# Projecting the v_s columns with the first chunk of w_in instead of with the last

## The chip, the core and the metric

The kernel runs on one core of a Trainium2 chip. The metric is the device time of one execution, in microseconds (us), as the median of several runs. TensorE is called PE here (PEld for its weight loads), VectorE DVE, ScalarE ACT, GpSimd POOL and SyncE SP.

## The reference, cut to what matters

Two transformer blocks over 512 tokens of width 1024: a block with sparse attention (NSA) and a gated MLP mixer plus a dense feed-forward part, then a block with differential attention and a mixture of 32 experts. The change concerns only the input projection of the first block:

```python
h = rms_norm(x, norm_mix_pre)                    # 512 x 1024
proj = jnp.einsum("bsd,de->bse", h, w_in)        # w_in is 1024 x 2328
q, k_c, v_c, k_s, v_s, k_w, v_w, gate_logits, u, v = jnp.split(proj, points, axis=-1)
# columns: q 0-511, k_c 512-639, v_c 640-767, k_s 768-895, v_s 896-1023,
#          k_w 1024-1151, v_w 1152-1279, gates 1280-1303, u 1304-1815, v 1816-2327
```

k_c and v_c are then compressed by small MLPs, and k_s, v_s, k_w, v_w and the gates go into the attention, with bias tables built from rel_bias.

## The kernel before

**Precision and splits.** Each fp32 operand is split into a high and a low fp32r part. ScalarE rounds a weight chunk from the ring buffer RING into WH (`act_split`), VectorE subtracts to get WL (`dve_split`), and PE sums three matmuls into a bank of PSUM (`pe_mm3`, L255 to L257: high x high, high x low, low x high).

**Chunks.** The weights of everything ahead of the experts come as a list of chunks (`front_chunks`). A chunk holds 4 k-tiles (512 of the 1024 rows) of some columns, so each set of columns is two chunks, which sum into the same banks. SyncE loads them in order into three slots of RING (`sp_load`, L218); a slot is reused when the chunk three before has been split (semaphore `w_lo`), or, for the raw chunks of the compression weights, when PE has consumed it (`p_blk`). Three pairs of WH and WL buffers hold the split chunks; a split waits for PE to have finished with the chunk that had the buffer (`p_pr`).

**The stage around the change** (`pe_win`, `act_win`, `dve_win`). The order on each engine is written out by hand. PE takes chunk 0 and 1 (k_c, v_c, k_s), 2 and 3 (q), 4 and 5 (k_w, then v_s, v_w and the gates), then the raw chunks 6 to 9 (L749: the compression's first layer), then 10 and on (u and v).

`pe_project` has two kinds of outputs. For kind "w" the weights are the stationary operand and the 512 tokens stream past: an output is 128 columns of w_in, transposed, and takes 4 k-tiles x 3 matmuls of 512 columns per chunk. For the other kind a block of 128 tokens is stationary and the weights stream: an output is 128 tokens x the columns, and takes 4 x 3 matmuls of as many columns as the set has. In chunks 4 and 5 the four outputs of the second kind have 280 columns: v_s, v_w and the gates (24).

**Biases.** The bias tables are made by tiny matmuls of 8 columns in bank 7: one far, four near groups of 64 (L627), four compressed groups of 31 (L634). `pe_project` takes a function `behind` that PE calls after each output; the bias groups stand there. A group waits until VectorE has copied the one before out of bank 7 (`v_bf`, L643; `v_bc`, L650).

**Leaving the banks.** ScalarE copies k_c and v_c out (L780) and starts DMAs that lay them out, copies k_s (L786, into KT4), starts more DMAs, splits chunks 4 and 5, and copies q (L799, bank 3 last) and k_w. VectorE copies v_s, v_w and gates together (L876, VSG). The first output of chunk 4 is k_w in bank 3, and waits for the last copy of q.

Of the kernel before, what the change touches and what calls it, by code (L numbers as in the profile page):

```python
# [59 lines left out]
def front_chunks():  # L60

    out = []

    def columns(src, cols, nout, nk=8, gain=None):
        for k0 in range(0, nk, 4):
            out.append(Chunk(src, k0, 4, cols, nout, gain=gain))

    def both(src, rows):
        for k0, nk in rows:
            for half in range(2):  # L70
                out.append(Chunk(src, k0, nk, [(512 * half, 512)], 4))

    columns("w_in", [(512, 384)], 3)
    columns("w_in", [(0, 512)], 4)
    columns("w_in", [(1024, 128), (896, 128), (1152, 152)], 5)
    for nm in ("cmp_w1_k", "cmp_w1_v"):
        for c in range(2):
            out.append(Chunk(nm, 8 * c, 8, [(0, 256)], 0, raw=True))
    columns("w_in", [(1304, 512)], 4)
    columns("w_in", [(1816, 512)], 4)  # L80
    both("w_out", ((4, 4), (0, 4)))
    for f in range(11):
        columns("w_gate_up", [(256 * f, 256), (FF + 256 * f, 256)], 4, gain=8)
    both("w_down", DOWN_ROWS)
    for grp in (0, 1, 3, 2):
        columns("w_in_2", [(grp * 512, 512)], 4, gain=16)
    both("w_out_2", ((4, 4), (0, 4)))

    loaded, outs, split, at, users = [0] * 3, 0, 0, 0, []
    for c, ch in enumerate(out):
        loaded[c % 3] += 16
        ch.slot, ch.loaded = c % 3, loaded[c % 3]
        ch.first_out = outs
        outs += ch.nout
        ch.done = outs
        ch.at, at = at, at + 128 * ch.nk * ch.w
        ch.split = None  # L100
        if not ch.raw:
            ch.split = split
            split += 1
            back = 3
            if ch.src == "w_out_2":
                if c == len(out) - 4:
                    users.append((users[-3][0], outs + 4))
                back = 2 if c == len(out) - 2 else 3
            ch.buf, ch.after = users[-back] if len(users) >= 3 else (split - 1, None)
            if c == len(out) - 1:  # L110
                ch.buf, ch.after = None, None

            users.append((ch.buf, outs + 2 if c == 16 else outs))
    return out
# [11 lines left out]
def program(nc, A):  # L126
    ctx = ExitStack()
    with ctx:
# [39 lines left out]
        def cols(off, a, n):  # L168
            return ar(off, a * n).rearrange("p (a n) -> p a n", a=a)
# [14 lines left out]
        for parts in (  # L184

                (("p_gt", 1), ("p_bf", 5), ("p_bc", 4)),

                (("p_kc", 1), ("p_vc", 1), ("p_gm", 8)),

                (("a_kct", 2), ("a_kts", 1), ("a_q", 4), ("a_kw", 1), ("a_hid", 2), ("a_sg", 1), ("a_u", 4), ("a_v", 4), ("a_lnv", 4)),  # L190

                (("a_lam", 1), ("a_rope", 2), ("a_sr", 1), ("a_gk", 1)),

                (("v_li", 1), ("v_gk", 1), ("v_ct", 1), ("v_cmpb", 1), ("v_eov", 1), ("v_sel", 1), ("v_blm", 1), ("v_dst", 1)),

                (("v_lam", 2), ("v_ang", 1), ("v_sr", 1)),

                (("v_gt", 1), ("v_t3", 1), ("v_bf", 5), ("v_bc", 4), ("v_blk", 8), ("v_vw", 4), ("v_hidr", 1), ("v_kc", 1), ("v_vc", 1), ("v_lnm", 1), ("v_wst", 2), ("v_zv", 1), ("v_gm", 8)),
        ):
            before = 0  # L200
            for name, count in parts:
                AT[name] = before
                before += count
# [316 lines left out]
        KT4 = cols(o, 4, 512); o_kt = o; o += 2048  # L520
        U = cols(o, 4, 512); o_u = o; o += 2048
        V = cols(o, 4, 512); o_v = o; o += 2048
        VSG = cols(o, 4, 280); o += 1120
        VS, VWG = VSG[:, :, 0:128], VSG[:, :, 128:280]
        BC = ar(o, 1024).rearrange("p (i h c) -> p i h c", i=4, h=8); o += 1024
        WK = ar(o, 3072); o_wk = o; o += 3072
        KC = ar(o, 64); o += 64
# [88 lines left out]
        def pe_bias_far(e):  # L616
            e.wait_ge(s("v_win"), AT["v_t3"] + 1)
            e.wait_ge(s("d_tb"), 64)
            e.wait_ge(s("v_xt"), XT["mix"] + 8)
            e.matmul(PS[7][:, 496:504], OH2[0:97, 711:712].broadcast_to([97, 128]), T3[0:97, 24:32], start=True, stop=True  # L620
                     ).then_inc(s("p_tab"), 1)
# [85 lines left out]

        def pe_win(e):
            xt = xt_of("mix")
            outs = [(n, PS[n][:, :], "w", n * 128, 128) for n in range(3)]  # L710
            pe_project(e, 0, outs, XP, 0, 8, {n: [("v_xt", XT["mix"] + n + 1)] for n in range(3)}, xt)

            def biases(e, o):
                if o == 0:
                    pe_bias_far(e)
                else:
                    pe_bias_near(e, o - 1)

            def more_biases(e, o):
                if o < 2:  # L720
                    pe_bias_near(e, o + 2)
                else:
                    pe_bias_cmp(e, o - 2)

            pe_project(e, 1, outs, XP, 4, 8, {}, xt, behind=biases)
            outs = [(m, PS[m][:, :], "w", m * 128, 128) for m in range(4)]
            free = {0: [("a_win", AT["a_kct"] + 1)], 1: [("a_win", AT["a_kct"] + 2)], 2: [("a_win", AT["a_kts"] + 1)]}

            def last_biases(e, o):
                if o < 2:  # L730
                    pe_bias_cmp(e, 2 + o)

            pe_project(e, 2, outs, XP, 0, 8, free, {}, behind=more_biases)
            pe_project(e, 3, outs, XP, 4, 8, {}, {}, behind=last_biases)
            outs = [(3, PS[3][:, :], "w", 0, 128)] + [(4 + i, PS[4 + i][:, 0:280], i, 128, 280) for i in range(4)]
            free = {3: [("a_win", AT["a_q"] + 4)], 7: [("v_win", AT["v_bc"] + 4)]}
            pe_project(e, 4, outs, XP, 0, 8, free, {})
            pe_project(e, 5, outs, XP, 4, 8, {}, {})

            for n in range(2):  # L740
                e.wait_ge(s("v_win"), AT["v_blk"] + 4 * n + 4)
                for c in (6 + 2 * n, 7 + 2 * n):
                    e.wait_ge(s(f"w_ld{CH[c].slot}"), CH[c].loaded)
                    for m in range(2):
                        if c % 2 == 0:
                            e.wait_ge(*((s("a_win"), AT["a_q"] + 1 + 2 * n + m), (s("a_win"), AT["a_kw"] + 1))[n * m])
                        for k in range(8):
                            k0 = 8 * (c % 2) + k
                            x = e.matmul(PS[2 * n + m][:, 0:62].rearrange("p (g c) -> p g c", g=2),  # L749
                                         RING[:, CH[c].slot, k * 256 + m * 128:k * 256 + (m + 1) * 128],  # L750
                                         BLK[n][:, k0, :, 0:31], start=(k0 == 0), stop=(k0 == 15))
                    x.then_inc(s("p_blk"), 1)

            def compressed_u(e, o):
                if o == 0:
                    pe_cmp_keys(e)
                elif o >= 2:
                    pe_cmp_logits(e, o - 2)

            def compressed_u2(e, o):  # L760
                if 1 <= o:
                    pe_cmp_values(e, o - 1)
                pe_cmp_T(e, o)
                if o < 2:
                    pe_cmp_logits(e, o + 2)

            def compressed_v(e, o):
                if o == 0:
                    pe_cmp_values(e, 3)

            pe_project(e, 10, full(H1), XP, 0, 8, {4 + i: [("v_win", AT["v_vw"] + 1 + i)] for i in range(4)}, {}, behind=compressed_u)
            pe_project(e, 11, full(H1), XP, 4, 8, {}, {}, behind=compressed_u2)
            pe_project(e, 12, full(H1), XP, 0, 8, {4 + i: [("a_win", AT["a_u"] + 1 + i)] for i in range(4)}, {}, behind=compressed_v)
            pe_project(e, 13, full(H1), XP, 4, 8, {}, {})

        def act_win(e):
# [7 lines left out]
                        e.dma_start(KK[n][64 * par:64 * par + 64, g, :], KCT[n][64 * g:64 * g + 64, :]).then_inc(s(f"d_kk{n}"), 16)  # L784
            e.wait_ge(s("p_pr"), CH[1].first_out + 3)
            e.activation(KT4[:, 0, :], PS[2][:, :], ACT.Copy).then_inc(s("a_win"), 1)  # L786
            e.wait_ge(s("a_win"), AT["a_kts"] + 1)
            for half in range(2):
                e.dma_start(KT4[64 * (1 - half):64 * (1 - half) + 64, 1, :], KT4[64 * half:64 * half + 64, 0, :]
                            ).then_inc(s("d_kts"), 16)  # L790
# [62 lines left out]
        def dve_win(e):  # L853
# [8 lines left out]
                                        ).then_inc(s("v_win"), 1)  # L862

            dve_bias_far(e)
            dve_split(e, 3)
            for kb in range(4):
                dve_bias_near(e, kb)
            for i in range(4):
                dve_bias_cmp(e, i)
# [3 lines left out]
            dve_split(e, 5)  # L873
            for i in range(4):
                e.wait_ge(s("p_pr"), CH[5].first_out + 2 + i)
                e.tensor_copy(VSG[:, i, :], PS[4 + i][:, 0:280]).then_inc(s("v_win"), 1)  # L876
            for n in range(2):
                e.memset(HID[n][:, :, :, 31:32], 0.0).then_inc(v_c.sem, v_c.up())
            e.memset(VC, 0.0).then_inc(v_c.sem, v_c.up())
# [2235 lines left out]
```

## Time and profile before

| | |
|---|---|
| median of 3 runs | 2118.25 us (2116.45 to 2121.68) |
| the profiled execution: its time | 2118.25 us |
| its span | 2116.4 us |
| PE busy | 2060.8 us (97%) |
| DVE busy | 1537.0 us (73%) |
| ACT busy | 1383.2 us (65%) |
| mean granted PE clock | 0.994 of full |
| all DMA | 511.27 MB, mean 242 GB/s |

Read it so: the span is from the first to the last instruction in the profile; the time has some 1.85 us around it. Busy is time with at least one instruction under way. Matmuls overlap, so a busy PE is not a PE at its peak, and the distance from one matmul's start to the next says more than a matmul's own duration. The stage of the change lies in the first 100 us.

### The profile page before, as it was taken

The page shows a single profiled execution, that of the slowest core. Times are in us where ns is not written, and L with a number is a line of the kernel's source. Part 1 is how long each engine was busy: PE and PEld are TensorE (multiplying, and loading weights), DVE is VectorE, ACT ScalarE, POOL GpSimd, SP SyncE. Part 2 cuts the span into 40 slices and gives each one's busy share as a digit, 9 for nine tenths or more (in the row PEclk, how much of TensorE's full clock was granted, in tenths as well). Part 3 has the DMA queues.
Part 4 walks back from the last instruction along what each step waited for, and adds up shares of the span by engine and source line. Part 5 has one row for each costly group of instructions (what it writes and reads, how often), then busy time and mean ns, then how long its engine had stood idle before and what let it go on. Part 6 is the DMA issues. An engine that isn't in the chain of part 4 may idle for free.

```text
span 2116.4 us, 31589 instructions
## 1 busy us (share of the span) xinstructions
PE 2060.8 (97%) x10497; PEld 1707.9 (81%) x10497; DVE 1537.0 (73%) x1825; ACT 1383.2 (65%) x1870; POOL 194.8 (9%) x232
## 2 busy tenths in 40 slices
PE   7998899999999999899999999999999999999998
PEld 6887788888887887778888888888888888888877
DVE  4357743332325677789899999989898989898984
ACT  3247643222323447478888888888888888888863
POOL 0000000000000000111111111111111111111110
PEclk9999999999999999999999999999999999999999
DMA  6321013222323311489999999999999999999971
GB/s 199 135 71 61 21 55 124 87 94 80 120 100 103 117 72 41 171 307 373 369 372 367 370 369 371 369 366 375 366 379 363 370 372 372 361 371 371 376 264 40
DMA packets 86560, 511.27 MB, mean 242 GB/s; under 512 B 17285, under 2 KB 18905, under 8 KB 29146
## 3 DMA queue, kind: packets, MB, share of 16 engines
q1 hardware_dynamic: 71312, 487.61, 61.2%
q0 software_dynamic: 9680, 17.33, 3.2%
q10 hardware_dynamic: 5498, 5.39, 0.9%
q8 instruction: 45, 0.74, 0.1%
q14 instruction: 25, 0.20, 0.0%
HBM read 503.44 MB, written 23.07 MB: 249 GB/s over the span
## 4 chain that ended last, share of the span: by engine, by line
PE 91%; DVE 5%; issue 1%; ACT 1%; DMA 1%; ACTq 0%; POOL 0%; DVEq 0%; SPq 0%; POOLq 0%
PE PS L2595 17%; PE PS L2597 17%; PE PS L2596 17%; PE PS L255 10%; PE PS L257 10%; PE PS L256 10%; PE PS L2478 1%; PE PS L2592 1%; PE PS L2605 1%; PE PS L1153 1%; PE PS L1865 1%; DVE AR L1124 1%; PE PS L1082 0%; PE PS L1800 0%; PE PS L1793 0%
## 5 line engine op out<-in xcount | busy, mean ns | idle before, releaser
L2472 DVE TENSOR_TENSOR WL<-RING,WH 128x2048 fp32r<-128x2048 f32 x385 | 873.5, 2288 | 95.6 <-ACT WH L2452 92.5
L2452 ACT ACTIVATE WH<-RING 128x1024 fp32r<-128x1024 f32 x770 | 806.4, 1059 | 163.1 <-PE PS L2597 157.5
L2595 PE MATMUL PS<-WH,RA 128*128 128x512 f32 x1540 | 628.5, 408 | 0.0
L2597 PE MATMUL PS<-WH,RA 128*128 128x512 f32 x1540 | 600.7, 390 | 0.0
L2596 PE MATMUL PS<-WL,RA 128*128 128x512 f32 x1540 | 600.4, 390 | 0.0
L2597 PEld LDWEIGHTS PS<-WH,RA 128*128 128x128 f32 x1540 | 289.5, 188 | 61.7
L2596 PEld LDWEIGHTS PS<-WL,RA 128*128 128x128 f32 x1540 | 289.9, 188 | 58.1
L2595 PEld LDWEIGHTS PS<-WH,RA 128*128 128x128 f32 x1540 | 290.8, 189 | 55.3
L255 PE MATMUL PS<-WH,RA 128*128 128x512 f32 (+1 forms) x560 | 219.4, 392 | 3.4 <-DVE WL L245 2.2
L257 PE MATMUL PS<-WH,RA 128*128 128x512 f32 (+1 forms) x560 | 216.1, 386 | 0.0
L256 PE MATMUL PS<-WL,RA 128*128 128x512 f32 (+1 forms) x560 | 215.8, 385 | 0.0
L250 DVE SCALAR_TENSOR_TENSOR WL<-RING,GT,WH 128x512 fp32r<-128x512 f32 x120 | 82.2, 747 | 167.7 <-ACT WH L235 167.6
L235 ACT ACTIVATE WH<-RING,GT 128x512 fp32r<-128x512 f32 x120 | 76.8, 713 | 175.2 <-PE PS L257 175.2
L255 PE MATMUL PS<-RA,WH 128*128 128x512 f32 (+1 forms) x448 | 168.7, 377 | 3.3 <-DVE RA L458 1.6
L256 PE MATMUL PS<-RA,WH 128*128 128x512 f32 (+1 forms) x448 | 167.6, 374 | 0.0
L257 PE MATMUL PS<-RA,WL 128*128 128x512 f32 (+1 forms) x448 | 167.6, 374 | 0.0
L245 DVE TENSOR_TENSOR WL<-RING,WH 128x2048 fp32r<-128x2048 f32 (+3 forms) x29 | 62.3, 2150 | 92.0 <-ACT WH L230 91.8
L255 PEld LDWEIGHTS PS<-WH,RA 128*128 128x128 f32 x560 | 105.7, 189 | 24.1 <-DVE WL L245 2.3
L257 PEld LDWEIGHTS PS<-WH,RA 128*128 128x128 f32 x560 | 105.7, 189 | 21.2
L256 PEld LDWEIGHTS PS<-WL,RA 128*128 128x128 f32 x560 | 105.8, 189 | 20.2 <-issue 0.2
L230 ACT ACTIVATE WH<-RING 128x2048 fp32r<-128x2048 f32 (+3 forms) x29 | 52.1, 1801 | 105.5 <-PE PS L257 95.9
L2757 POOL DMA_INDIRECT acc_scr<-AR,SMALL x32 | 69.9, 2185 | 464.8 <-issue 464.8
(395 smaller groups left out, 2265.9 us busy)
## 6 DMA issues: line engine op xcount, KB each, us to landing
RING<-w_experts SPq DMA_DIRECT2D x390, 1024.0 KB, 7.3
RING<-w_front SPq DMA_DIRECT2D x58, 1024.0 KB, 4.9
X<-x SPq DMA_DIRECT2D x4, 512.0 KB, 5.6
acc_scr<-X SPq DMA_DIRECT2D x4, 512.0 KB, 5.0
xs_scr<-AR SPq DMA_DIRECT2D x4, 512.0 KB, 3.1
X<-acc_scr SPq DMA_DIRECT2D x4, 512.0 KB, 5.5
out<-X SPq DMA_DIRECT2D x8, 256.0 KB, 2.0
RING<-w_front SPq DMA_DIRECT2D x2, 816.0 KB, 4.4
```

The costliest lines, as they stand in the source:

```text
L235: x = e.activation(WH[:, ch.buf, v], RING[:, ch.slot, v], ACT.Copy, scale=GT[:, g:g + 1])
L245: x = e.tensor_tensor(WL[:, ch.buf, 0:n], RING[:, ch.slot, 0:n], WH[:, ch.buf, 0:n].bitcast(F32), ALU.subtract)
L250: x = e.scalar_tensor_tensor(WL[:, ch.buf, v], RING[:, ch.slot, v], GT[:, g:g + 1], WH[:, ch.buf, v].bitcast(F32), ALU.mult, ALU.subtract)
L255: e.matmul(out, a[0], b[0], start=start, stop=False)
L256: e.matmul(out, a[0], b[1], start=False, stop=False)
L257: return e.matmul(out, a[1], b[0], start=False, stop=stop)
L2452: e.activation(WH[:, m % 3, v], RING[:, m % 6, v], ACT.Copy).then_inc(s("m_hi"), 1)
L2472: e.tensor_tensor(WL[:, m % 3, :], RING[:, m % 6, :], WH[:, m % 3, :].bitcast(F32), ALU.subtract).then_inc(s("m_lo"), 1)
L2595: e.matmul(PS[bank][:, :], lhs[0][:, kr + k, :], WH[:, m % 3, c], start=(sel is None and kr == 0 and k == 0), stop=False)
L2596: e.matmul(PS[bank][:, :], lhs[0][:, kr + k, :], WL[:, m % 3, c], start=False, stop=False)
L2597: x = e.matmul(PS[bank][:, :], lhs[1][:, kr + k, :], WH[:, m % 3, c], start=False, stop=(stop and k == 3))
L2757: e.indirect_dma_start(acc_d, bass.IndirectOffsetOnAxis(TCOL, 0), YY, None, bounds_check=511, oob_is_err=False, compute_op=ALU.add).then_i ...
```

## The change

The v_s columns (896 to 1023) move into chunks 0 and 1, which grow from 384 to 512 columns; chunks 4 and 5 shrink from 408 to 280. Chunks 0 and 1 get four more outputs each, of the second kind, 128 columns wide, in banks 3 to 6. The outputs of that kind in chunks 4 and 5 shrink from 280 to 152 columns (v_w and the gates). Chunk 1 now has seven outputs, and seven of the bias groups stand behind them (far, four near, two compressed); the last two compressed ones stand behind chunk 2. ScalarE copies v_s out in four copies after that of k_s; VectorE's copies in chunk 5 are 152 wide. VectorE copies the first near group before it splits chunk 3. VS and VWG are now tiles of their own.

```diff
-    columns("w_in", [(512, 384)], 3)
+    columns("w_in", [(512, 512)], 7)
     columns("w_in", [(0, 512)], 4)
-    columns("w_in", [(1024, 128), (896, 128), (1152, 152)], 5)
+    columns("w_in", [(1024, 280)], 5)
...
-(("a_kct", 2), ("a_kts", 1), ("a_q", 4), ...
+(("a_kct", 2), ("a_kvs", 5), ("a_q", 4), ...
...
-        VSG = cols(o, 4, 280); o += 1120
-        VS, VWG = VSG[:, :, 0:128], VSG[:, :, 128:280]
+        VS = cols(o, 4, 128); o += 512
+        VWG = cols(o, 4, 152); o += 608
...
-            outs = [(n, PS[n][:, :], "w", n * 128, 128) for n in range(3)]
-            pe_project(e, 0, outs, XP, 0, 8, {n: [("v_xt", XT["mix"] + n + 1)] for n in range(3)}, xt)
+            outs = ([(n, PS[n][:, :], "w", n * 128, 128) for n in range(3)]
+                    + [(3 + i, PS[3 + i][:, 0:128], i, 384, 128) for i in range(4)])
+            pe_project(e, 0, outs, XP, 0, 8, {n: [("v_xt", XT["mix"] + n + 1)] for n in range(7)}, xt)

             def biases(e, o):
                 if o == 0:
                     pe_bias_far(e)
+                elif o < 5:
+                    pe_bias_near(e, o - 1)
                 else:
-                    pe_bias_near(e, o - 1)
-
-            def more_biases(e, o):
-                if o < 2:
-                    pe_bias_near(e, o + 2)
-                else:
-                    pe_bias_cmp(e, o - 2)
+                    pe_bias_cmp(e, o - 5)
...
-            free = {0: [("a_win", AT["a_kct"] + 1)], 1: [("a_win", AT["a_kct"] + 2)], 2: [("a_win", AT["a_kts"] + 1)]}
+            free = {0: [("a_win", AT["a_kct"] + 1)], 1: [("a_win", AT["a_kct"] + 2)], 2: [("a_win", AT["a_kvs"] + 1)], 3: [("a_win", AT["a_kvs"] + 2)]}
...
-            pe_project(e, 2, outs, XP, 0, 8, free, {}, behind=more_biases)
-            pe_project(e, 3, outs, XP, 4, 8, {}, {}, behind=last_biases)
-            outs = [(3, PS[3][:, :], "w", 0, 128)] + [(4 + i, PS[4 + i][:, 0:280], i, 128, 280) for i in range(4)]
-            free = {3: [("a_win", AT["a_q"] + 4)], 7: [("v_win", AT["v_bc"] + 4)]}
+            pe_project(e, 2, outs, XP, 0, 8, free, {}, behind=last_biases)
+            pe_project(e, 3, outs, XP, 4, 8, {}, {})
+            outs = [(3, PS[3][:, :], "w", 0, 128)] + [(4 + i, PS[4 + i][:, 0:152], i, 128, 152) for i in range(4)]
+            free = {4 + i: [("a_win", AT["a_kvs"] + 3 + i)] for i in range(3)}
+            free.update({3: [("a_win", AT["a_q"] + 4)], 7: [("v_win", AT["v_bc"] + 4)]})
...
             e.activation(KT4[:, 0, :], PS[2][:, :], ACT.Copy).then_inc(s("a_win"), 1)
-            e.wait_ge(s("a_win"), AT["a_kts"] + 1)
+            for i in range(4):
+                e.wait_ge(s("p_pr"), CH[1].first_out + 4 + i)
+                e.activation(VS[:, i, :], PS[3 + i][:, 0:128], ACT.Copy).then_inc(s("a_win"), 1)
+            e.wait_ge(s("a_win"), AT["a_kvs"] + 1)
...
             dve_bias_far(e)
+            dve_bias_near(e, 0)
             dve_split(e, 3)
-            for kb in range(4):
+            for kb in range(1, 4):
                 dve_bias_near(e, kb)
...
-                e.tensor_copy(VSG[:, i, :], PS[4 + i][:, 0:280]).then_inc(s("v_win"), 1)
+                e.tensor_copy(VWG[:, i, :], PS[4 + i][:, 0:152]).then_inc(s("v_win"), 1)
```

## Rows read from the trace of the kernel before

**Rows 1.** The page's chain that ended last: share of the span by engine.

```profile
PE 91%; DVE 5%; issue 1%; ACT 1%; DMA 1%; ACTq 0%; POOL 0%; DVEq 0%; SPq 0%; POOLq 0%
```

**Rows 2.** Chain that ended last, 0 to 120 us: start, us, engine, tile, line.

```profile
18.31 0.47 PE PS L255
...
67.33 0.61 ACT AR L799
68.08 0.47 PE PS L255
...
86.22 7.10 PE PS L749 x64
93.34 4.98 DMA RING<-w_front
98.35 1.92 ACT WH L230
100.29 2.30 DVE WL L245
102.64 0.80 PE PS L255
103.43 0.43 PE PS L256
...
108.71 0.89 PE PS L931 x8
```

**Rows 3.** Timeline of PE, chunks 4 and 5: start, us, line, tile, shapes.

```profile
70.92 0.28 PE L255 MATMUL PS<-WH,RA 128*128 128x280 f32 x1
...
77.09 0.40 PE L255 MATMUL PS<-RA,WH 128*128 128x512 f32 x1
77.32 0.39 PE L256 MATMUL PS<-RA,WH 128*128 128x512 f32 x1
```

**Rows 4.** Timeline of PE, transposes of an expert.

```profile
926.11 0.60 PE L2605 MATMUL PS<-CST,AR 128*128 128x128 f32 x4
```

**Rows 5.** Timeline of PE, two fp32r matmuls of 128 columns in the attention.

```profile
162.14 0.22 PE L1147 MATMUL PS<-RA 128*128 128x128 f32 x1
162.20 0.28 PE L1148 MATMUL PS<-RA 128*128 128x128 f32 x1
```

**Rows 6.** Weight loads by line and form: count | busy us, mean ns.

```profile
L256 PEld LDWEIGHTS PS<-WL,RA 128*128 128x128 f32 x560 | 105.8, 189 | 20.2 <-issue 0.2
...
L749 PEld LDWEIGHTS PS<-AR,RING 128*128 128x128 f32 x128 | 14.4, 192 | 0.0
...
L627 PEld LDWEIGHTS PS<-AR 97*128 97x128 bf16 x256 | 6.7, 96 | 1.0 <-issue 1.0
```

**Rows 7.** Timeline around the first near-bias group.

```profile
32.20 1.76 PE L627 MATMUL PS<-AR 97*128 97x8 bf16 x64
...
33.82 0.48 PE L255 MATMUL PS<-RA,WH 128*128 128x512 f32 x1
...
34.09 0.68 DVE L643 COPY RING<-PS 128x512 f32<-128x512 f32 x1
```

**Rows 8.** Timeline of VectorE, its split of chunk 4.

```profile
66.04 1.86 DVE L245 TENSOR_TENSOR WL<-RING,WH 128x1632 fp32r<-128x1632 f32 x1
```

**Rows 9.** DMA issues between 2.9 and 3.3 us: count, KB, us to landing.

```profile
RING<-w_front SPq DMA_DIRECT2D x1, 768.0 KB, 8.1
```

**Rows 10.** Timeline of VectorE, first activation tiles.

```profile
17.42 5.36 DVE L334 SCALAR_TENSOR_TENSOR RA<-PS,GT,RA 128x512 fp32r<-128x512 f32 x8 [1.60 <-ACT RA L327]
```

**Rows 11.** Stretches: engines busy (x instructions), PEclk, DMA share, GB/s.

```profile
86.00:93.30 7.30, 7.30 (x68) 7.30 (x66) 0.96 (x4) 0.00 (x0) 0.00 (x0) 1.00 0.37 120
...
98.20:101.60 3.40, 2.26 (x21) 2.12 (x20) 1.31 (x1) 3.00 (x4) 0.00 (x0) 1.00 0.86 299
101.60:108.40 6.80, 5.76 (x15) 4.65 (x16) 3.61 (x3) 5.32 (x5) 0.00 (x0) 0.50 0.86 318
```

More of the change, by code:

```diff
@@ L188, in program @@
                 (("p_kc", 1), ("p_vc", 1), ("p_gm", 8)),
-                (("a_kct", 2), ("a_kts", 1), ("a_q", 4), ("a_kw", 1), ("a_hid", 2), ("a_sg", 1), ("a_u", 4), ("a_v", 4), ("a_lnv", 4)),
+                (("a_kct", 2), ("a_kvs", 5), ("a_q", 4), ("a_kw", 1), ("a_hid", 2), ("a_sg", 1), ("a_u", 4), ("a_v", 4), ("a_lnv", 4)),
                 (("a_lam", 1), ("a_rope", 2), ("a_sr", 1), ("a_gk", 1)),
```

## The prediction

> **What bounds the kernel now.** I read the page first: the chain that ended last is 91% PE [rows 1]. So what matters is whether the edited stretch lies on that chain, and there the chain in order of time is the view to read [rows 2]. From 18.31, the first matmul of chunk 0, it runs through PE alone to 93.34, with one step aside: at 67.33 ScalarE reads bank 3 (0.61 us) before chunk 4 may write it. At 86.22 begin the compression matmuls of L749. When they have consumed the ring's chunk 7, SyncE issues the load of chunk 10 (4.98 us), ScalarE and VectorE split it (1.92 and 2.30 us), and PE goes on at 102.64. The reader should see two things. The load that holds PE up at 93 to 103 us is itself started by PE, so PE work added before 86.22 moves everything behind it one for one. And no other engine has to be made faster here: up to 93.34 the chain never passes through VectorE.
>
> Then I read single matmuls, start to start, because their busy times overlap. 512 columns go at 0.23 us. The 48 matmuls of 280 columns go from 70.92 to 77.09, which is 6.17 / 48 = 0.1285 us each [rows 3]. The 280-column ones are in the "x" outputs of chunks 4 and 5, where activations are the stationary operand: a new 128x128 weight load for each.
>
> **The change part by part.** (a) v_s (128 columns of w_in) moves from chunks 4 and 5 to chunks 0 and 1. The bytes over the six chunks, and the columns computed, are the same. But the matmuls are not: before, v_s shared its matmuls with v_w and the gates (280 columns). After, chunks 0 and 1 get 4 outputs x 4 k-tiles x 3 terms x 2 chunks = 96 more matmuls of 128 columns, and the 96 of 280 columns become 96 of 152. PE issues 96 more weight loads and as many matmuls, for no more columns.
>
> What a narrow fp32r matmul with a new weight tile costs is the disputed price; the trace has no long row of them. Plain fp32 instructions with new 128x128 weights go at 7.10 / 64 = 0.111 us with 62 columns, 0.89 / 8 = 0.111 us with 64 columns [rows 2], and 4 transposes of 128 columns take 0.60 us [rows 4], of which 0.28 is the time of the last by itself (a lone 128-column matmul's in [rows 5]): (0.60 - 0.28) / 3 = 0.11 us. Width makes no difference there, so something other than the streamed columns sets 0.111. The weight load is the candidate: its record is 192 ns for fp32 and 189 ns for the fp32r loads of the projection, but 96 ns for bf16 [rows 6], and bf16 pairs go at 1.60 / 64 = 0.025 us, as the near-bias group of L627 shows [rows 2]. fp32r weights load like fp32 weights, so I take 0.111 us for 128 and for 152 columns. The ends: from above 0.1285, since fewer columns with the same load should not take longer than 280 do. From below 0.06: in the attention one fp32r matmul of 128 columns is followed by another with other weights after 162.20 - 162.14 = 0.06 us [rows 5]. That is a single pair after a 512-column matmul, whose length hid the first load, so it does not show a stream; the long rows are nearer to the case.
>
> Added: 96 x 0.111 = +10.7 us. Saved: 96 x (0.1285 - 0.111) = -1.7 us. Net +9.0 us on PE. With 0.1285 for both it is +12.3.
>
> A rule of the Trainium skill would price this lower: TensorE: Matmul & The Clock Gate, section Back-to-back issue gap, gives about 81 ns for each pair of weight load and matmul at 128 columns in a sustained stream. By it the sum would be 96 x 0.081 - 96 x (0.1285 - 0.081) = +3.2 us. The fp32 rows at 0.111 us speak against it; no row here shows it for fp32r.
>
> (b) The bias matmuls are re-hung. The far one, four near and four compressed groups still run, each as long as before: behind chunks 1 and 2 rather than 1, 2 and 3. Their PE time is unchanged (a near group is 33.82 - 32.20 = 1.62 us [rows 7]). What could be new is a wait for bank 7: VectorE must copy a group away before the next. The copy begins at 34.09 and ends at 34.77, 0.95 us after the group made way for L255 at 33.82 [rows 7]. Before, an output of 12 x 0.23 = 2.7 us stood between groups; now, from the fourth output on, an output of 12 narrow matmuls does, 12 x 0.111 = 1.33 us. That still covers 0.95, so I cost it at 0. If the narrow ones ran at 0.06 the cover would be 0.72 us, and some 0.25 us would be lost at each of three hand-offs. VectorE's first near copy is moved ahead of its split of chunk 3 for this; that split is wanted only when chunk 3 begins, with all of chunk 2, 48 x 0.23 = 11 us, still between.
>
> (c) ScalarE copies v_s out of banks 3 to 6, four copies of 128 columns (0.61 us is what it takes for 512 [rows 2]), between chunk 1's outputs. Queued behind them on its queue are two key-copy DMAs, three loads of the compression's second weights, and the split of chunk 4. The split's WL half is wanted by PE when chunk 4 starts, with chunks 2 and 3 between, 96 x 0.23 = 22 us; the DMAs' data later. Cost 0. Chunk 2 writes bank 3 as its fourth output, long after that bank's copy.
>
> (d) The wait before chunk 4. Chunk 4 starts at 68.08, because of the bank 3 copy (67.33 + 0.61). VectorE's split of chunk 4 ended at 66.04 + 1.86 = 67.90 [rows 8], as late as the copy. After the change this split is earlier (the last bias copy before it is two outputs further ahead of chunk 3, and the chunk is smaller), but the bank stays: chunk 4 still writes bank 3 first. Gain 0; at most 0.9 us if both went.
>
> (e) The start. Chunks 0 and 1 grow from 768 KB to 1 MB each. Chunk 0 is issued at about 3.0 and lands 8.1 us later, at 11.1 [rows 9]. Behind x (2 MB) it came at no less than (2 + 0.75) MB in 11.1 us, so 256 KB more are at most 1.0 us. Its split is the first step that could feel it. VectorE's split of 512 columns more (2048 take 2.30 us [rows 2]) adds 0.6 us, and VectorE idled 1.60 us between this split and its first activation tile at 17.42 [rows 10]. I take it as hidden; if the load and both splits (0.5 us on ScalarE too) all came on top, 2.1 - 1.6 = 0.5 us would show.
>
> **Sum.** +10.7 - 1.7 + 0 = +9.0 us. The profiled execution took 2118.25 us (span 2116.4 and 1.85 around it), which is also the median of the three runs, so 2127.3 us, 0.43% more. About 0.3% (6.4 us) is what a measurement of this kernel can tell from no change.
>
> **The rivals.** Partly covered loads: the spacing is between the two ends, say (0.06 + 0.111) / 2 = 0.085 us, because part of a load runs under the matmul ahead. Then 96 x 0.085 = 8.2, less 96 x (0.1285 - 0.085) = 4.2: +4.0 us, 2122.3. The one pair at 0.06 is for it; the groups at 0.111 are against. The 81 ns of the Trainium skill's page TensorE: Matmul & The Clock Gate would make this the case.
>
> Narrow matmuls at stream rate, which is the case on the other side (not slower): 0.06 us for 128 columns and 0.06 x 152 / 128 = 0.071 for 152. Added 5.8, saved 96 x 0.0575 = 5.5, hand-offs 0.75: +1.1 us, 2119.3. It decides from a spacing of 0.098 us down, where 96 x (2 x spacing - 0.1285) falls under the 6.4 us named above. For it speaks the same pair, against it the equal 0.111 at 62, 64 and 128 columns.
>
> The clock falls in the new stretch. Around chunk 1's last outputs PE would now do nothing but bias groups of 8 columns and narrow matmuls for some 9 us. The granted clock was 1.00 at 86 to 93.3, nearly all 62-column instructions, but 0.50 (1.2 of 2.4 GHz) at 101.6 to 108.4, behind 98.2 to 101.6 in which PE was busy 2.26 of 3.40 us with such instructions [rows 11]. At 0.50 the 512-column matmuls go at 0.43 us rather than 0.23 [rows 2], and about 13 of them passed before the clock came back: 13 x 0.20 = 2.6 us. So +11.6 us, 2129.9. Against: the clock stayed at 1.00 under seven us of 62-column work [rows 11]. The spell at 101.6 itself could also shift or vanish, 2.6 us less: 2124.7; this belongs to the spread of the forecast.
>
> The added work is hidden: the sum would be 0 if something else ended last in this stretch. The chain passes through nothing but PE from 18.31 to 67.33 and again from 68.08 to 93.34 [rows 2], so I give it almost nothing.
>
> **Numbers.** Forecast (0.111 us, spread 2124.7 to 2130): 0.65. Clock falls: 0.12. Partly covered: 0.10. Stream rate: 0.10. Anything else, a gain in a later stage included: 0.03. The range 2120.5 to 2131 takes in all but the stream-rate case and the outliers. Slower by over 0.3%: nearly all of the first, all of the second, a little of the third, 0.76. Within: 0.20. Faster: 0.04.
>
> **What would show it.** In the trace after: 96 matmuls of 128 columns in chunks 0 and 1 spaced 0.11 us, so chunk 1 begins about 48 x 0.111 = 5.3 us later; L749's 64-group begins at about 95.3 rather than 86.22, chunk 10's first matmul at about 111.7. The 152-column ones are spaced 0.11 too. No PE wait over 0.1 us on VectorE's bias copies; granted clock 1.00 between 16 and 95 us. The prediction is wrong if the spacing of the 128-column matmuls is under 0.09 us, if PE waits at bank 7 or for a split, or if the distance of 9 us between the two traces at L749 is gone by the end.

## The result, and the profile after

The changed kernel takes 2136.1 us (median of 4 runs, 2132.85 to 2138.85) against 2119.47 (2116.45 to 2121.68): ratio 1.0081, 95% interval 1.0065 to 1.0096, so 14 to 20 us slower. A second comparison gave 1.0075 (1.006 to 1.009). I had forecast 9.0 us, with 2131 as the upper end of the range.

The page of the kernel after: the chain that ended last is PE's as before [rows 1].

```profile
PE 91%; DVE 4%; issue 2%; DMA 1%; ACT 1%; ACTq 0%; POOL 0%; SPq 0%; DVEq 0%; POOLq 0%
```

The chain in order of time, to be held against [rows 2]:

```profile
18.11 0.47 PE PS L255
...
42.02 1.60 PE PS L627 x64
45.01 1.60 PE PS L627 x64
...
49.27 1.73 PE PS L627 x64
...
57.99 0.63 PE PS L255
58.62 0.43 PE PS L256
...
64.45 0.23 PE PS L256
...
84.21 0.61 ACT AR L800
...
101.42 7.15 PE PS L747 x64
108.58 5.23 DMA RING<-w_front
...
118.13 0.79 PE PS L255
```

L747 (L749 before) begins at 101.42 instead of 86.22: 15.2 us late, where I expected 9. The distance is made by then, ahead of the load of chunk 10 and everything behind it; chunk 10's first matmul, at 118.13, is 15.5 us late. The row to stop at is 58.62: a 512-column matmul of chunk 2 that takes 0.43 us, and it is back to 0.23 at 64.45.

The stretches of the kernel after (columns as in [rows 11]) say why:

```profile
16.20:46.60 30.40, 29.45 (x335) 25.72 (x333) 17.50 (x24) 12.34 (x15) 0.00 (x0) 1.00 0.51 150
46.60:63.80 17.20, 17.20 (x199) 15.71 (x199) 2.28 (x5) 1.97 (x4) 0.00 (x0) 0.51 0.13 28
63.80:101.40 37.60, 36.82 (x250) 31.96 (x246) 12.05 (x15) 5.42 (x7) 0.00 (x0) 1.00 0.20 64
```

The granted clock is 1.00 to 46.6, about 0.5 for 17.2 us (the 1.2 GHz level), and 1.00 again up to L747. PE is busy all through the middle stretch. In the kernel before, the clock is 1.00 throughout this part:

```profile
26.50:48.00 21.50, 21.50 (x323) 18.00 (x322) 9.06 (x17) 5.27 (x5) 0.00 (x0) 1.00 0.67 193
48.00:67.20 19.20, 19.20 (x194) 15.46 (x192) 6.69 (x11) 3.36 (x4) 0.00 (x0) 1.00 0.00 1
```

The narrow matmuls, on PE's timeline in chunk 0 of the kernel after. They answer to [rows 3] and [rows 5]:

```profile
26.40 0.22 PE L255 MATMUL PS<-WH,RA 128*128 128x128 f32 x1
26.46 0.28 PE L256 MATMUL PS<-WL,RA 128*128 128x128 f32 x1
26.57 0.27 PE L257 MATMUL PS<-WH,RA 128*128 128x128 f32 x1
26.68 0.27 PE L255 MATMUL PS<-WH,RA 128*128 128x128 f32 x1
...
31.71 0.45 PE L255 MATMUL PS<-RA,WH 128*128 128x512 f32 x1
```

48 matmuls of 128 columns take 31.71 - 26.40 = 5.31 us, 0.111 us each. The first pair stands 0.06 us apart, just as the pair of [rows 5] did, and from the second on it is 0.11: such a pair behind a wide matmul did not show what a run of them costs.

The hand-off of bank 7, on the timeline of the kernel after, the counterpart of [rows 7]:

```profile
41.86 1.76 PE L627 MATMUL PS<-AR 97*128 97x8 bf16 x64
...
43.48 0.31 PE L255 MATMUL PS<-WH,RA 128*128 128x128 f32 x1
...
43.65 0.69 DVE L643 COPY RING<-PS 128x512 f32<-128x512 f32 x1 [1.43 <-PE PS L627]
...
44.85 1.76 PE L627 MATMUL PS<-AR 97*128 97x8 bf16 x64
```

The near group at 41.86 gives way to a narrow output at 43.48, VectorE's copy runs from 43.65 to 44.34, and the next group starts at 44.85, when that output is through. PE never waits for the bank.

### The profile page after: what moved, and what is told of

It is laid out like the page before. It is cut to its first block, busy times and chain, and to the rows that moved or that the text cites. A ratio compares the mean times of both kernels' runs of the same rounds, so it can differ in the third digit from the quotient of the medians.

```text
span 2138.6 us, 31785 instructions
## 1 busy us (share of the span) xinstructions
PE 2081.3 (97%) x10593; PEld 1727.7 (81%) x10593; DVE 1537.0 (72%) x1825; ACT 1384.6 (65%) x1874; POOL 194.7 (9%) x232
## 4 chain that ended last, share of the span: by engine, by line
PE 91%; DVE 4%; issue 2%; DMA 1%; ACT 1%; ACTq 0%; POOL 0%; SPq 0%; DVEq 0%; POOLq 0%
PE PS L2597 16%; PE PS L2599 16%; PE PS L2598 16%; PE PS L255 10%; PE PS L257 10%; PE PS L256 10%; PE PS L2480 1%; PE PS L2594 1%; PE PS L2607 1%; PE PS L1155 1%; PE PS L1867 1%; DVE AR L1126 1%; PE PS L1084 1%; DMA AR<-ffn_norm 0%; PE PS L1795 0%
## 5 line engine op out<-in xcount | busy, mean ns | idle before, releaser
L2599 PEld LDWEIGHTS PS<-WH,RA 128*128 128x128 f32 x1540 | 289.6, 188 | 61.8
L2597 PEld LDWEIGHTS PS<-WH,RA 128*128 128x128 f32 x1540 | 290.9, 189 | 57.6 <-issue 2.2
L2598 PEld LDWEIGHTS PS<-WL,RA 128*128 128x128 f32 x1540 | 290.2, 188 | 58.2
L255 PE MATMUL PS<-WH,RA 128*128 128x512 f32 (+2 forms) x592 | 229.4, 387 | 3.6 <-DVE WL L245 2.4
L257 PE MATMUL PS<-WH,RA 128*128 128x512 f32 (+2 forms) x592 | 226.0, 382 | 0.0
L256 PE MATMUL PS<-WL,RA 128*128 128x512 f32 (+2 forms) x592 | 225.8, 382 | 0.0
L255 PEld LDWEIGHTS PS<-WH,RA 128*128 128x128 f32 x592 | 113.6, 192 | 24.5 <-DVE WL L245 2.6
L257 PEld LDWEIGHTS PS<-WH,RA 128*128 128x128 f32 x592 | 113.7, 192 | 21.1
L256 PEld LDWEIGHTS PS<-WL,RA 128*128 128x128 f32 x592 | 113.8, 192 | 20.2 <-issue 0.2
L245 DVE TENSOR_TENSOR WL<-RING,WH 128x2048 fp32r<-128x2048 f32 (+2 forms) x29 | 62.3, 2150 | 92.8 <-ACT WH L230 92.7
L230 ACT ACTIVATE WH<-RING 128x2048 fp32r<-128x2048 f32 (+2 forms) x29 | 52.1, 1802 | 110.7 <-PE PS L257 101.6
```

The costliest lines, as they stand in the source:

```text
L245: x = e.tensor_tensor(WL[:, ch.buf, 0:n], RING[:, ch.slot, 0:n], WH[:, ch.buf, 0:n].bitcast(F32), ALU.subtract)
L255: e.matmul(out, a[0], b[0], start=start, stop=False)
L256: e.matmul(out, a[0], b[1], start=False, stop=False)
L257: return e.matmul(out, a[1], b[0], start=False, stop=stop)
L2597: e.matmul(PS[bank][:, :], lhs[0][:, kr + k, :], WH[:, m % 3, c], start=(sel is None and kr == 0 and k == 0), stop=False)
L2598: e.matmul(PS[bank][:, :], lhs[0][:, kr + k, :], WL[:, m % 3, c], start=False, stop=False)
```

## The experiments

Each is told by where its run of L747's 64 instructions begins (86.22 before, 101.42 after), by the granted clock up to there, and by its ratio to the kernel before. The first four share one set of runs of the kernel before, the other four another. The first matmul of chunk 0 does not start at the same time in every trace (18.31 before); where that matters, it is said.

**The biases where they were, the narrow matmuls kept.** On the changed kernel, with `more_biases` as it was before the change:

```diff
-                elif o < 5:
-                    pe_bias_near(e, o - 1)
-                else:
-                    pe_bias_cmp(e, o - 5)
+                elif o < 3:
+                    pe_bias_near(e, o - 1)
...
-            pe_project(e, 2, outs, XP, 0, 8, free, {}, behind=last_biases)
-            pe_project(e, 3, outs, XP, 4, 8, {}, {})
+            pe_project(e, 2, outs, XP, 0, 8, free, {}, behind=more_biases)
+            pe_project(e, 3, outs, XP, 4, 8, {}, {}, behind=last_biases)
```

> The changed kernel with its bias groups back where they were before the change: far and two near groups behind the wide outputs of chunk 1, the others behind chunks 2 and 3; the 96 added matmuls of 128 columns stay. Theory A (two costs: the added weight loads, 9.0 us, and a clock spell of about 6 us that comes from narrow matmuls and bias groups standing side by side): the granted clock stays at 1.00 up to L747, whose 64-group begins near 95.3 us (before 86.2, after 101.4), and the time is 9 to 10 us over the kernel before, near 2128. Rival B (the clock falls from the narrow matmuls alone, wherever the biases are): a stretch at 0.50 in chunk 0 or 1 again, L747 near 99 to 101, time near 2134. Rival C (the loss of 15 us has nothing to do with the order of the biases): L747 at 101, time as the changed kernel's 2136.

Measured: 2129.96 us, median of 6 runs (one of them took 2141.94), ratio 1.0058 (1.0038 to 1.0079). Its chain and its stretches:

```profile
78.81 0.47 PE PS L255
...
102.45 5.61 DMA RING<-w_front
```

```profile
26.50:48.00 21.50, 21.50 (x253) 19.41 (x253) 8.58 (x14) 4.38 (x7) 0.00 (x0) 1.00 0.53 154
48.00:79.00 31.00, 30.22 (x360) 24.96 (x360) 9.12 (x14) 5.11 (x8) 0.00 (x0) 1.00 0.08 17
79.00:95.30 16.30, 16.30 (x122) 15.25 (x122) 5.14 (x8) 1.88 (x2) 0.00 (x0) 1.00 0.46 146
95.30:102.50 7.20, 7.20 (x67) 7.20 (x66) 0.83 (x4) 0.05 (x1) 0.00 (x0) 1.00 0.37 117
```

The clock is 1.00 in all four stretches, and the load of chunk 10 starts at 102.45 instead of 93.34: 9.1 us later. Chunk 4 starts at 78.81 instead of 68.08, 10.7 us later, which is the forecast's term for the added matmuls; the narrower chunks 4 and 5 give 1.6 back. The order of the biases alone is worth 6 us of the 15; with it undone, what is left is the 9.0 us of the forecast.

**The weight loads alone.** The kernel before, with every 280-column matmul issued as one of 128 and one of 152 columns:

```diff
+                if cw == 280:
+                    for k in range(ch.nk):
+                        n = n0 + k
+                        for q0, qw in ((0, 128), (128, 152)):
+                            i = pe_mm3(e, out[:, q0:q0 + qw], ..., n == 0 and q0 == 0, n == nk - 1 and q0 > 0)
```

> The kernel before with each of its 96 matmuls of 280 columns issued as one of 128 and one of 152 with the same weights loaded twice, in chunks 4 and 5, with no bias group near: the added weight loads alone. Theory A (each narrow fp32r matmul with its weight load takes 0.111 us): 96 x (2 x 0.111 - 0.1285) = 9.0 us more, L749 at 95.2 instead of 86.2, clock 1.00 up to there, time near 2128. Rival B (narrow matmuls in a long run bring the clock down by themselves; here 192 of them, 21 us, run on end into the 62-column ones): L749 at 95 but a stretch at 0.50 in it, 100 us or later, time 2131 to 2140. Rival C (a second matmul on the same weights is cheaper): under 5 us.

Measured: 2129.51 us, ratio 1.005 (1.0036 to 1.0064). Its chain, where L759 is the old L749:

```profile
95.25 7.14 PE PS L759 x64
102.41 5.17 DMA RING<-w_front
```

L759 begins at 95.25, 9.03 us later than before; 96 x (2 x 0.111 - 0.1285) is 8.98. This is the cost of chunks 4 and 5 alone, for chunk 4 starts at 68.06 here and at 68.08 before. The clock was 1.00 from 68 to 102 us. In that time 96 narrow matmuls ran on end for 10.7 us, then the 12 of 512 columns with which chunk 5 begins (81.58 to 84.4), then 96 narrow ones again and the 62-column ones; the expectation overlooked the wide ones between. So 96 more weight loads cost 9 us in either place, and a run of 96 narrow matmuls by itself did not bring the clock down. A single run of all 192, as rival B has it, was not tried.

**More columns for nothing.** The changed kernel with its 128-column matmuls widened to 256, of which half is used:

```diff
-                    + [(3 + i, PS[3 + i][:, 0:128], i, 384, 128) for i in range(4)])
+                    + [(3 + i, PS[3 + i][:, 0:256], i, 256, 256) for i in range(4)])
...
-                e.activation(VS[:, i, :], PS[3 + i][:, 0:128], ACT.Copy).then_inc(s("a_win"), 1)
+                e.activation(VS[:, i, :], PS[3 + i][:, 128:256], ACT.Copy).then_inc(s("a_win"), 1)
```

> The changed kernel with its 96 matmuls of 128 columns widened to 256 (k_s and v_s together; the v_s half is used), bias groups as in the changed kernel. More columns stream for nothing. Theory A (the clock falls because the array streams little in that stretch): each matmul takes 0.120 us instead of 0.111, 0.9 us more, but the granted clock stays at 1.00 or falls for less, L747 between 96 and 100 instead of 101.4, time 2129 to 2134, less than the changed kernel's 2136. Rival B (the number of weight loads or of instructions brings the clock down, not the columns): a stretch of 17 us at 0.50 as before, L747 at 102.5 to 104, time 2137 or more.

Measured: 2131.09 us, ratio 1.005 (1.0038 to 1.0063), where the changed kernel has 1.0081 and 1.0075. Its chain, its stretches, and two matmuls on its timeline:

```profile
95.96 7.15 PE PS L747 x64
```

```profile
32.00:60.00 28.00, 28.00 (x458) 24.90 (x457) 8.66 (x10) 5.95 (x9) 0.00 (x0) 1.00 0.35 93
60.00:96.00 36.00, 35.22 (x232) 30.61 (x231) 11.62 (x15) 5.41 (x7) 0.00 (x0) 1.00 0.21 66
```

```profile
45.06 0.28 PE L257 MATMUL PS<-WH,RA 128*128 128x256 f32 x1
45.18 0.28 PE L255 MATMUL PS<-WH,RA 128*128 128x256 f32 x1
```

The matmuls take 0.12 us instead of 0.111, the bias groups stand exactly where the change puts them, and the clock stays at 1.00. L747 begins at 95.96: 0.7 us behind the run with the split 280s, and 5.5 us ahead of the changed kernel. Work that is thrown away made the stage faster. The medians lie 5 to 6 us apart too; the interval lies below the changed kernel's first one and just touches the second. The number of instructions and of weight loads is that of the changed kernel (rival B of this run is out); what differs is that the 96 matmuls stream twice the columns and stand 0.12 us apart. There is one trace of this kernel, but its six runs have mean clocks of 0.991 to 0.994 against 0.985 to 0.991 of the changed kernel. The width of single instructions is not the whole account: the 62-column ones keep 1.00 in every trace here.

**Biases in a run, no narrow fp32r matmuls.** The kernel before, with three near and two compressed groups behind chunk 1's last output (the last two compressed ones behind chunk 2, and VectorE's first near copy ahead of its split of chunk 3, both as in the change):

```diff
-                else:
-                    pe_bias_near(e, o - 1)
+                elif o == 1:
+                    pe_bias_near(e, 0)
+                else:
+                    for kb in range(1, 4):
+                        pe_bias_near(e, kb)
+                    for i in range(2):
+                        pe_bias_cmp(e, i)
```

> The kernel before (no v_s move, no added matmuls) with near groups 1 to 3 and compressed groups 0 and 1 in one run behind chunk 1's last output. PE waits for VectorE's copy of bank 7 between them, about 1 us four times, 4 us. Theory A (bias groups in a run bring the clock down even without narrow fp32r matmuls): a stretch at 0.50 from about 42 us on, chunk 2's first matmuls of 512 columns at 0.43 us, L749 at 90 plus 2 to 5 us. Rival B (it takes the narrow fp32r matmuls): clock 1.00, L749 at 90, time near 2122.

Measured: 2125.64 us, ratio 1.0029 (1.0019 to 1.0039). Its chain and its stretches:

```profile
48.27 0.43 PE PS L256
...
92.77 7.10 PE PS L748 x64
```

```profile
36.00:40.00 4.00, 3.21 (x105) 2.82 (x105) 1.56 (x2) 0.60 (x1) 0.00 (x0) 0.99 0.80 199
40.00:53.70 13.70, 10.92 (x203) 9.12 (x199) 2.28 (x5) 1.56 (x1) 0.00 (x0) 0.51 0.28 75
53.70:73.00 19.30, 19.30 (x116) 15.93 (x113) 12.13 (x12) 3.37 (x4) 0.00 (x0) 1.00 0.30 103
```

The clock falls here too, at 40.0 for 13.7 us, without one narrow fp32r matmul. PE stands idle 0.8 + 2.8 = 3.6 us in the first two stretches (the hand-offs of bank 7), and the 12 matmuls of chunk 2's first output go at 0.43 us, 2.4 us more; L748 is 92.77 - 86.22 = 6.5 us late. So the narrow fp32r matmuls are not needed for a fall (rival B of this run is out). But PE was idle for part of the time here, which it was not in the changed kernel, and no run shows the bias groups without these waits.

**VectorE's order.** The changed kernel with chunk 3's split ahead of the first near copy again:

```diff
-            dve_bias_near(e, 0)
             dve_split(e, 3)
-            for kb in range(1, 4):
+            for kb in range(4):
```

> The changed kernel with VectorE's order of before: chunk 3's split ahead of the first near copy. Theory (this edit is a hand-off detail): PE waits up to about 2 us more for bank 7 at the second near group (split of 2.3 us ahead of the copy, less the 2.7 us output between), nothing else; the spell at 0.50 stays, L747 between 101 and 104. Rival (the edit is part of the loss): L747 earlier than 101.

One run, 2141.07 us. Its chain:

```profile
101.31 7.15 PE PS L747 x64
```

101.31 against 101.42, with the spell (the stretch at the lower clock) in place: in this one trace the edit is worth nothing, not even the wait that I had allowed for. The second near group starts at 41.74, right behind its output (41.86 in the changed kernel).

**The changed kernel once more.** No edit.

> The changed kernel itself once more, as the control of this call and for a second trace. Theory (the spell belongs to the kernel's order of work and comes in every run, as the clock means of 0.986 to 0.991 in its seven runs suggest): again a stretch at 0.50 that begins between 43 and 48 us and ends by 65, L747 near 101; ratio to the kernel before 1.0065 to 1.0096. What differs after 850 us between the first two traces (5 us in the router stage) is a spell that varies from run to run, so the distance to before at the end should not be 22 us again. Rival (the spell was an accident of one execution): clock 1.00 to L747, L747 at 95, time near 2128.

Measured: 2137.17 us, ratio 1.0075 (1.006 to 1.009). Its stretches:

```profile
32.00:45.00 13.00, 13.00 (x214) 11.14 (x214) 5.97 (x4) 3.06 (x5) 0.00 (x0) 0.99 0.56 151
45.00:62.00 17.00, 17.00 (x203) 15.79 (x200) 2.28 (x5) 1.97 (x4) 0.00 (x0) 0.50 0.16 38
62.00:100.00 38.00, 37.22 (x267) 32.25 (x265) 12.04 (x15) 5.41 (x7) 0.00 (x0) 1.00 0.20 63
```

```profile
100.36 7.15 PE PS L747 x64
```

The spell comes again, from 45 to 62, and before it PE was busy 13.00 of 13.00 us. L747 is 14.1 us late; the first matmul stands at 17.21 here, 1.1 us ahead of before, so from there to L747 it is 15.2. The seven runs of the changed kernel in the first comparison have mean clocks of 0.986 to 0.991, and the six here 0.985 to 0.991; the kernel before has 0.990 to 0.995 in its 32 runs of the two calls. The spell belongs to the kernel, not to one execution. At its end this trace lies 20.6 us behind the one of before; I had expected it not to be 22 us again.

**The same work, thinned.** The changed kernel with near groups 2 and 3 behind the second and fourth narrow output, none behind the first and third, and all compressed groups behind chunk 2:

```diff
-                elif o < 5:
+                elif o < 3:
                     pe_bias_near(e, o - 1)
-                else:
-                    pe_bias_cmp(e, o - 5)
+                elif o % 2 == 0:
+                    pe_bias_near(e, o // 2)
...
-                if o < 2:
-                    pe_bias_cmp(e, 2 + o)
+                pe_bias_cmp(e, o)
```

> The changed kernel with its last four narrow outputs of chunk 1 less crowded: near groups 2 and 3 behind the second and the fourth of them, none behind the first and the third, and all four compressed groups behind chunk 2's outputs. Between the second and the last wide output of the stage PE still does only narrow work, 5.3 us of matmuls and 3.2 us of bias groups instead of 5.3 and 4.8. Theory (too little streamed in a stretch brings the clock down; less bias work between narrow matmuls means less of it): no spell or one of 3 to 7 us, L747 at 95.3 to 98. Rival (any mixture of narrow matmuls with bias groups does it): a spell as long as before, L747 at 100 or later.

Measured: 2133.29 us, ratio 1.0066 (1.0051 to 1.0082). Its chain and stretches:

```profile
97.31 7.15 PE PS L746 x64
```

```profile
42.00:49.60 7.60, 7.60 (x161) 7.60 (x158) 1.38 (x2) 1.38 (x4) 0.00 (x0) 0.99 0.48 159
49.60:56.40 6.80, 6.80 (x81) 6.05 (x81) 0.76 (x2) 1.41 (x2) 0.00 (x0) 0.51 0.33 71
56.40:97.00 40.60, 39.82 (x332) 34.18 (x331) 12.84 (x17) 5.41 (x7) 0.00 (x0) 1.00 0.18 59
```

A spell of 6.8 us instead of 17, and L746 at 97.31, 11.1 us late: 9 for the loads, 2 for the clock. With less bias work between the narrow outputs there is less of the spell, as the trace shows; the time's interval overlaps that of the changed kernel. The edit also brings chunk 2's wide matmuls forward, to 52.8 from 57.9, so this run does not tell a less crowded stretch from a shorter one.

**A version that uses the gap.** Built on the kernel before, v_s left where it was: the compressed bias groups run behind L749's last group, where PE waits for chunk 10, in banks 0 and 1; k_w goes to bank 7 and the last 280-column output to bank 3. VectorE copies the compressed groups out after its split of chunk 6.

```diff
+        VB = (4, 5, 6, 3)
...
-            outs = [(3, PS[3][:, :], "w", 0, 128)] + [(4 + i, PS[4 + i][:, 0:280], i, 128, 280) for i in range(4)]
+            outs = [(7, PS[7][:, :], "w", 0, 128)] + [(VB[i], PS[VB[i]][:, 0:280], i, 128, 280) for i in range(4)]
...
                     x.then_inc(s("p_blk"), 1)
+            for i in range(4):
+                pe_bias_cmp(e, i)
```

> Built on the kernel before, with v_s left where it was. The four compressed bias groups run where PE waits for chunk 10 anyway (behind L749's last group, in banks 0 and 1), and k_w goes to bank 7 instead of bank 3, so that chunk 4 need not wait for the copy of q. Theory: 3.1 us of bias groups and 0.4 us of restarts leave the path ahead of L749, the wait of 0.9 us before chunk 4 goes, and about 0.9 us comes back at chunk 10, since the groups take 3.1 us and the gap has 2.2. Sum: L749 begins at 86.2 - 4.4 = 81.8 us, chunk 10 at 102.6 - 3.5 = 99.1, and the time is about 3.5 us under the kernel before, 2115.7, which is within what a measurement can tell. Rival (the spell at 0.50 around chunk 10 gets longer, as PE now does 8-column work just before it): chunk 10's distance is eaten up again, time as before.

Measured: 2115.65 us, median of 11 runs, against 2119.54: ratio 0.9982, 95% interval 0.9973 to 0.9991. Its chain and PE's timeline:

```profile
81.46 14.24 PE PS L744 x128
...
98.86 0.63 PE PS L255
```

```profile
95.53 3.32 PE L635 MATMUL PS<-AR 97*128 97x8 bf16 x124
98.72 0.77 PE L255 MATMUL PS<-WH,RA 128*128 128x512 f32 x1
```

L744 begins at 81.46 (4.8 us earlier than before), the four compressed groups take 3.3 us from 95.53, and chunk 10 starts at 98.86 instead of 102.64, 3.8 us earlier. Of both, 0.3 us is an earlier first matmul (17.99), which leaves 4.4 and 3.5 as expected. The spell around chunk 10 is as long as before, 6.8 us at 0.50 from 97.6, so the rival of this run is out. The gain of 0.18% is small but its interval does not reach 1, and it is the only kernel of these that beats the one before. The two edits were not run apart.

## Why the prediction was wrong

- **The chain lies in PE alone, so work added ahead of L749 moves everything:** right. The 15.2 us at L747 are 15.5 at chunk 10, and still 15.2 at the last matmul of L1802 (866.2 us; 851.0 before, as L1800); in the run with the biases back, 9.1 us at the load behind L751.
- **(a) 0.111 us for a narrow fp32r matmul with new weights, +9.0 us:** right. Chunk 0's 48 took 0.111 us each; the split of the 280s alone cost 9.03 us, and the changed kernel without the spell 9.1. The rivals of partly covered loads and of the stream rate are out. For the rule of the Trainium skill weighed there (TensorE: Matmul & The Clock Gate, Back-to-back issue gap: about 81 ns), the runs disagree: 111 ns for fp32r in a run.
- **(b) the bias groups cost the same and the hand-off is covered:** right in what it says of waits: PE goes from the output straight into the next group, and VectorE's order made no difference. But the step priced the edit at 0, and that is where the missing 6 us were made: not by a wait, but by what the neighbourhood does to the clock.
- **(c), (e) ScalarE's copies and the larger first chunks are hidden:** right. The first matmul starts at 18.11 (18.31 before).
- **(d) the wait before chunk 4 stays:** right, the chain still passes through ScalarE's copy at 84.21, for 0.61 us.
- **The rival "the clock falls in the new stretch": this is what happened,** in every traced execution of the changed kernel, and I had given it 0.12. This is the step that failed, twice. Its chance was set by comparing the stretch with the 62-column instructions, which had kept 1.00 for 7 us. But between them stood no groups of 8 columns; the two kinds of small matmuls side by side are a different stretch, which the trace of before nowhere shows. And its price was taken from the spell at 101.6 to 108.4, 2.6 us, as if a spell had one length. This one lasted 17 us: it began while the narrow outputs still ran and went on through chunk 2's first output. In its rows: 36 narrow matmuls at 0.213 us rather than 0.111, +3.7 us (the last three narrow outputs, timeline below); 12 wide ones at 0.43 rather than 0.23, +2.4 us; the groups inside it 0.3 (49.27 in the chain is 1.73 long, 1.60 at full clock). Together 6.4 us. From the first matmul to L747 it is 83.31 us, and 67.91 before: 15.4, which is 9.0 + 6.4; the 15.2 at L747 have an earlier start by 0.2 in them. The narrow output behind the third near group, on the timeline of the kernel after, with ten spacings of 2.13 / 10 us:

```profile
46.72 0.41 PE L256 MATMUL PS<-WL,RA 128*128 128x128 f32 x1
...
48.85 0.41 PE L257 MATMUL PS<-WH,RA 128*128 128x128 f32 x1
```

With the right price on that rival the sum is 9.0 + 6.4 = 15.4 us, 2133.7, inside the measured 14 to 20. Two things stay open. One is what in that stretch makes the granted clock fall: with the bias groups moved back there is no spell, with the matmuls widened there is none, and bias groups with waits bring one without narrow fp32r matmuls, but no run goes further. The other is the rest, 1 to 2 us of the median: the two traces of the changed kernel lie 22 and 21 us behind the one of before at the end, but their further 5 to 7 us arise behind 866 us, mostly in the router stage near 900 us and at the very end. The kernel before has spells there too: from 880 to 935 us its mean granted clock is 0.88, and 0.75 and 0.81 in the two traces of the changed kernel. No run here separates chance from consequence in that part.

## What to carry to other kernels

Cutting a set of columns out of a matmul whose stationary operand changes each time is not free of cost: each further matmul with its weight load took 0.111 us here at 128 and at 152 columns, and 256 columns only 0.12, so keep such outputs wide. Tiny matmuls stood best spread between wide ones; before moving them, look at what PE streams on both sides of them and not only at whether somebody waits, and ask of each spell of low clock how long it would last behind the new order. And an engine's gap on the critical path (here the load of chunk 10) is the place for such small work.

## What the runs showed of the hardware

- fp32r matmuls with new 128x128 weights go at 0.111 us with 128 and 152 columns, 0.12 with 256, 0.1285 with 280 and 0.23 with 512: from 128 to 152 columns the width did not count, and up to 256 hardly. Only the first pair behind a wide matmul stands 0.06 us apart.
- The granted clock fell to its lower level while PE was busy without a gap (13.00 of 13.00 us before the fall in the second trace, 17.20 of 17.20 behind it in the first), and stayed at 1.00 when its 128-column matmuls were 256 wide. PE being busy was not enough to keep the clock.
- It stayed at 1.00 under 96 narrow fp32r matmuls on end (10.7 us), and under the 128 fp32 ones of 62 columns on end (14.24 us, in the last experiment).
- At the lower level a 128-column fp32r matmul with its weight load takes 0.213 us, a 512-column one 0.43, but a near group of 64 tiny bf16 ones 1.73 against 1.60 us.
